# The decode rows' projection on four column strips in fp32, head norms in pairs, and attention's transfers later

## The reference

```
kv = einsum('btd,de->bte', rms_norm(x, g_kv), w_kv)      # 1024 x 3072: k and v of 3 groups, 8 heads of 64
k, v = rotary(rms_norm(kv[:, :, 0], k_gain), pos), kv[:, :, 1]
q = einsum('btd,de->bte', rms_norm(x, g), w_q)           # 1024 x 1536
q = rotary(rms_norm(q, q_gain), pos) * 64 ** -0.5        # rms_norm here is over each head of 64
o_g, lse_g = softmax attention of group g: windows 128, 512, 2048, dilations 1, 4, 16
o = sum_g softmax_g(lse_g) * o_g;  x = x + o @ w_o
```

## Time and profile before

| | |
|---|---|
| median of three runs | 2099.83 us |
| the profiled execution | 2097.21 us, span 2095.4 us |
| its mean granted TensorE clock | 0.993 of full speed |
| TensorE's busy share of the span | 99% |
| chain that ended last, share on TensorE | 92% (VectorE 4%, DMA 1%, ScalarE 1%) |
| HBM traffic | 303.02 MB read, 172.30 MB written |

### The profile page before, as it was taken

The page is one execution under the profiler, slowest core; times in us unless marked ns, Lnnn a source line. Parts: engine busy times, 40 slices in busy tenths (PEclk is TensorE's granted clock), DMA queues, the critical chain, the costliest instruction groups (busy, mean ns, idle before and its releaser), DMA issues.

```text
span 2095.4 us, 44747 instructions
## 1 busy us (share of the span) xinstructions
PE 2065.7 (99%) x17325; PEld 2011.4 (96%) x17325; DVE 1596.1 (76%) x2141; ACT 1083.3 (52%) x1963; POOL 562.9 (27%) x630
## 2 busy tenths in 40 slices
PE   8999999999999999999999899999999999999998
PEld 8999999999999999999999767899999999999998
DVE  5888888888755787867868697788888888875544
ACT  5655555455544665455554456555555555553332
POOL 1002232322210254635546203620132322321000
PEclk8999999999999999999999999999999999999999
DMA  6235777788998632453534785122676878899664
GB/s 209 82 102 160 201 188 208 192 198 213 302 291 261 204 121 91 129 158 108 188 127 143 238 242 200 35 92 86 166 194 193 211 187 213 191 300 295 195 207 141
DMA packets 264468, 380.67 MB, mean 182 GB/s; under 512 B 23511, under 2 KB 161399, under 8 KB 262438
## 3 DMA queue, kind: packets, MB, share of 16 engines
q1 hardware_dynamic: 227670, 281.35, 41.5%
q0 software_dynamic: 31376, 92.79, 20.3%
q10 hardware_dynamic: 5288, 4.68, 0.7%
HBM read 303.02 MB, written 172.30 MB: 227 GB/s over the span
## 4 chain that ended last, share of the span: by engine, by line
PE 92%; DVE 4%; DMA 1%; ACT 1%; issue 1%; POOL 0%; SPq 0%; ACTq 0%; DVEq 0%; POOLq 0%
PE ps L1290 42%; PE ps L1393 21%; PE ps L2607 5%; PE ps L2609 5%; PE ps L2610 5%; PE ps L2861 2%; PE ps L2924 2%; PE ps L2626 2%; PE ps L2960 1%; PE ps L2939 1%; PE ps L446 1%; PE ps L889 1%; PE ps L2887 1%; PE ps L512 1%; PE ps L2916 1%; DMA chin<-in_state_conv 1%
## 5 line engine op out<-in xcount | busy, mean ns | idle before, releaser
L1290 PE MATMUL ps<-hT,w 128*128 128x258 f32 x2752 | 458.3, 283 | 0.5 <-DVE ua L1523 0.5
L1290 PEld LDWEIGHTS ps<-hT,w 128*128 128x128 f32 x2752 | 384.9, 189 | 1.2 <-issue 0.6
L1290 PE MATMUL ps<-lT,w 128*128 128x258 f32 x1376 | 276.2, 282 | 0.0
L1290 PE MATMUL ps<-hB,w 128*128 128x258 f32 x1344 | 229.4, 282 | 0.0
L1290 PEld LDWEIGHTS ps<-lT,w 128*128 128x128 f32 x1376 | 213.3, 189 | 0.0
L1393 PE MATMUL ps<-gdh,wda 128*128 128x258 f32 x1184 | 198.8, 283 | 0.0
L1393 PE MATMUL ps<-gdh,wdb 128*128 128x258 f32 x1152 | 193.4, 284 | 0.0
L1290 PEld LDWEIGHTS ps<-hB,w 128*128 128x128 f32 x1344 | 191.0, 189 | 0.0
L1393 PEld LDWEIGHTS ps<-gdh,wda 128*128 128x128 f32 x1184 | 166.8, 190 | 0.3
L1393 PEld LDWEIGHTS ps<-gdh,wdb 128*128 128x128 f32 x1152 | 161.7, 189 | 0.8 <-issue 0.2
L2607 PE MATMUL ps<-ring,xhS 128*128 128x256 f32 x560 | 157.8, 282 | 0.0
(11 more groups left out here) (414 smaller groups left out, 5579.5 us busy)
## 6 DMA issues: line engine op xcount, KB each, us to landing
stage<-in_w_up SPq DMA_DIRECT2D x176, 256.0 KB, 3.6
wsum<-in_w_down POOLq DMA_DIRECT2D x132, 256.0 KB, 5.3
gs<-cb SPq DMA_DIRECT2D x44, 516.0 KB, 6.9
stage<-wsum SPq DMA_DIRECT2D x88, 256.0 KB, 3.3
tsum<-gs POOLq DMA_DIRECT2D x66, 258.0 KB, 7.5
tsum<-gneg POOLq DMA_DIRECT2D x66, 258.0 KB, 8.5
stage<-in_w_down SPq DMA_DIRECT2D x58, 256.0 KB, 3.4
kvs<-stage SPq DMA_DIRECT2D x24, 512.0 KB, 4.4
```

Source lines behind the costliest of these rows:

```text
L1290: mm = pe.matmul(ps[:, bank + c, 0:HB], w, m[:, c * HB:(c + 1) * HB], start=(first and i == 0), stop=(i == len(parts) - 1), skip_group_che ...
```

## The change

Four parts.

1. The samples' rows are multiplied in plain fp32: xs and xs12 hold the 8 rows once, and the moving operand is the scaled but unsplit weights in their own buffers (`raw`). The four 128-row parts of a block go to four column strips (`strip_products`), so one block is 4 matmuls of 32x256, and each strip keeps its own partial sum. `samples_first` does B11 ahead of that product, `samples` does B21, T3 and B22 together behind T1 (in step 0 behind B21). ScalarE copies the strips out (`act_strips`), `fold_samples` adds them on TensorE by four matmuls with a summing matrix inside product T3, and VectorE copies 4 pieces (`dve_sample_rows`). Since `raw` is read by the matmuls, the sum T1 of step n now waits for the B11 strips (`samples_begun`), and the load of the next B12 for all strips.
2. Norms are done in pairs: c11 and c22 share floor, root and the four small operations, so do c12 and c21. The scaling of the first of a pair moves behind the second's sum.
3. In the last step the first q tile is copied earlier and the masks are built later.
4. In attention, loads of cache rows (`V_AT`) are spread over s = 3 to 13 in place of 2 to 9 and 13; copies of k/v rows to outputs move from s = 4 on to s = 16 on, the loads of x from s = 10 on to s = 14 on; `sp_new_rows` is cut in two, and its loads for the samples move from s = 3 to s = 4.

```diff
@@ -2270,11 +2293,23 @@
             wait(act, pj_cs, 2 * n - 1)
             act_wide(act, two(rb[:, 0:T]), ps[:, 2:4, :], (pj_pe, nth(n, "T3")))
 
-        def act_sample_low(act, n):
-            act.wait_ge(pj_ss, n + 3)
-            row_free(act, n, "S")
-            wait(act, pj_k, 2 * n)
-            nc.scalar.activation(knS[:, :], ps[32:XS, 6 + n % 2, :], ACT.Copy).then_inc(pj_k, 1)
+        def samples_done(n):
+            return (pj_ss, 3 * n + 3)
+
+        def samples_folded(n):
+            return (pj_ss, 3 * n + 4)
+
+        def samples_begun(n):
+            return (pj_ss, 3 * n + 2)
+
+        def kept_strips(n):
+            return xb12[:, 0:QW] if n == LASTP else strips[:, :]
+
+        def act_strips(act, n):
+            act.wait_ge(*samples_done(n))
+            if n == LASTP:
+                act.wait_ge(pj_l, nth(n, "T3"))
+            nc.scalar.activation(kept_strips(n), ps[:, 6 + n % 2, :], ACT.Copy).then_inc(pj_xh, 1)
 
         def act_project(act):
             def act_x_his(name):
...
@@ -2363,32 +2396,39 @@
             row_free(v, n, "c12")
             nc.vector.tensor_tensor(two(row(n, "c12")), ps[:, 4:6, :], two(acc[:, 0:T]), ALU.add).then_inc(pj_cs, 1)
 
-        def dve_sample_add(v, n):
-            v.wait_ge(pj_k, 2 * n + 1)
-            nc.vector.tensor_tensor(knS[:, :], knS[:, :], ps[0:NS, 6 + n % 2, :], ALU.add).then_inc(pj_k, 1)
+        def dve_sample_rows(v, n):
+            v.wait_ge(*samples_folded(n))
+            row_free(v, n, "S")
+            for q in range(4):
+                ins = nc.vector.tensor_copy(knS[:, q * P:(q + 1) * P], ps[32 * q:32 * q + NS, 6 + n % 2, q * P:(q + 1) * P])
+            ins.then_inc(pj_k, 1)
 
...
@@ -2440,29 +2479,33 @@
                     if before:
                         dve_mean(v, n - 1, "c12")
                         dve_lo(v, n, "B21")
-                        dve_normed(v, n - 1, "c12")
-                        dve_sample_add(v, n - 1)
+                        dve_sample_rows(v, n - 1)
                         dve_lo(v, n, "T3")
                         if last:
                             dve_weights_sum(v, n, "T4")
                         dve_mean(v, n - 1, "c21")
+                        dve_floor(v, n - 1, "near")
+                        if last:
+                            dve_lo(v, n, "T4")
+                        else:
+                            dve_lo(v, n + 1, "B11")
+                        dve_factor(v, n - 1, "near")
+                        dve_normed(v, n - 1, "c12")
+                        dve_mean(v, n - 1, "S")
+                        dve_floor(v, n - 1, "rows")
                         dve_normed(v, n - 1, "c21")
                         if last:
-                            dve_lo(v, n, "T4")
-                        dve_mean(v, n - 1, "S")
-                        if not last:
-                            dve_lo(v, n + 1, "B11")
+                            dve_first_queries(v)
+                        dve_factor(v, n - 1, "rows")
                         dve_normed(v, n - 1, "S")
                         if not normed:
                             sample_scores(v, gi, 0)
...
@@ -2473,31 +2516,31 @@
                     dve_weights_sum(v, n + 1, "T1")
                 if normed:
                     dve_mean(v, n, "c11")
-                    dve_normed(v, n, "c11")
                 dve_c22p(v, n)
                 if not last:
                     dve_weights_sum(v, n, "T4")
                     dve_lo(v, n, "T4")
                 if n == 0:
                     dve_x_los("A22")
-                if last:
-                    v.wait_ge(at_tp, 1)
-                    nc.vector.tensor_scalar(qT[:, 0, :], ps[:, 7, :], gq[:, 0:1], None, ALU.mult).then_inc(at_tc, 1)
                 if normed:
                     dve_mean(v, n, "c22")
+                    dve_floor(v, n, "far")
+                    dve_factor(v, n, "far")
+                    dve_normed(v, n, "c11")
                     dve_normed(v, n, "c22")
                 else:
                     dve_values(v, n, "c22")
                 if last:
                     v.wait_ge(at_tp, 2)
                     nc.vector.tensor_copy(kT[:, 0, :], ps[:, 7, :]).then_inc(at_tc, 1)
+                    dve_masks(v)
...
-            def samples(n, b):
-
-                rows = {"B11": xs[:, 0:KH, :], "B21": xs[:, KH:KC, :], "T3": xs[:, 0:KH, :], "B22": xs12[:, :, :]}[b]
-                h, first = (0 if b in ("B11", "B21") else 1), b in ("B11", "T3")
-                w = wslot(n, b)
-                pe.wait_ge(pj_l, nth(n, b))
-                if b == "B11" and n:
-                    pe.wait_ge(*((pj_k, 2 * n - 2) if n > 1 else (pj_s, 2)))
+            def strip_products(n, b, rows, h, moving):
+                for k in range(KH):
+                    mm = pe.matmul(ps[32 * k:32 * k + XS, 6 + n % 2, h * CW:(h + 1) * CW], rows[:, k, :],
+                                   moving[:, k * CW:(k + 1) * CW], start=(b == "B11"), stop=(b in ("B21", "B22")),
+                                   tile_position=(0, 32 * k), skip_group_check=True)
+                return mm
+
+            def samples_first(n):
+
                 if n == 0:
-                    pe.wait_ge(pj_xs, {"B11": 3, "B21": 5, "T3": 3, "B22": 6}[b])
-                for k in range(KH):
-                    for i in range(2):
-                        mm = pe.matmul(ps[0:XS, 6 + n % 2, h * CW:(h + 1) * CW], rows[:, k, :], w[:, i, k * CW:(k + 1) * CW],
-                                       start=(b == "B11" and k == 0 and i == 0), stop=(not first and k == KH - 1 and i == 1),
-                                       skip_group_check=True)
-                if b == "B22":
-                    mm.then_inc(pj_ss, 1)
-                return mm
+                    pe.wait_ge(pj_xh, 1)
+                    pe.wait_ge(pj_l, nth(0, "B11"))
+                    w = wslot(0, "B11")
+                    strip_products(0, "B11", xs[:, 0:KH, :], 0, w[:, 0, :].bitcast(F32))
+                    mm = strip_products(0, "low", xs[:, 0:KH, :], 0, w[:, 1, :].bitcast(F32))
+                else:
+                    pe.wait_ge(*scaled_by(n, "B11"))
+                    pe.wait_ge(*((pj_k, n - 1) if n > 1 else (pj_s, 2)))
+                    mm = strip_products(n, "B11", xs[:, 0:KH, :], 0, raw(n, "B11"))
+                mm.then_inc(pj_ss, 1)
+
+            def samples(n):
+                if n == 0:
+                    pe.wait_ge(pj_xh, 2)
+                    pe.wait_ge(pj_xs, 4)
+                pe.wait_ge(*scaled_by(n, "B21"))
+                pe.wait_ge(*weights_summed(n, "T3"))
+                strip_products(n, "B21", xs[:, KH:KC, :], 0, raw(n, "B21"))
+                strip_products(n, "T3", xs[:, 0:KH, :], 1, raw(n, "T3"))
+                strip_products(n, "B22", xs12, 1, raw(n, "B22")).then_inc(pj_ss, 1)
+
+            def fold_samples(n):
+                pe.wait_ge(pj_xh, 2 + n + 1)
+                for q in range(4):
+                    mm = pe.matmul(ps[32 * q:32 * q + NS, 6 + n % 2, q * P:(q + 1) * P], fold[:, :],
+                                   kept_strips(n)[:, q * P:(q + 1) * P], start=True, stop=True, tile_position=(0, 32 * q),
+                                   skip_group_check=True)
+                mm.then_inc(pj_ss, 1)
 
             pe.wait_ge(f_xa, 6 * KH + 1)
             product(0, "B11")
             pe.wait_ge(f_xa, 7 * KH)
             for c in range(2):
                 pe.matmul(ps[:, 2 + c, :], xq["A11"][0][:, 0, 0:P], pre0[:, 0, 0:QW], start=True, stop=True)
-            samples(0, "B11").then_inc(pj_ss, 1)
+            samples_first(0)
             for n in range(LASTP + 1):
                 wait(pe, pj_cs, 2 * n)
                 product(n, "T1")
@@ -2645,18 +2708,19 @@
                         nm = pe.matmul(ps[0:MT[i], 7, i:i + 1], acc[:, i * P:i * P + MT[i]], ones[:, 0:1],
                                        start=True, stop=True)
                     nm.then_inc(pj_ss, 1)
+                if n:
+                    samples(n)
                 pe.wait_ge(pj_cp, 5 * n + 1)
                 product(n, "T2")
-                samples(n, "B21")
                 product(n, "B21")
-                samples(n, "T3")
+                if n == 0:
+                    samples(n)
                 pe.wait_ge(pj_cp, 5 * n + 2)
-                product(n, "T3")
+                product(n, "T3", third=lambda: fold_samples(n))
                 if n < LASTP:
-                    samples(n + 1, "B11")
+                    samples_first(n + 1)
                     pe.wait_ge(pj_cp, 5 * n + 3)
                     product(n + 1, "B11")
-                    samples(n, "B22")
                     pe.wait_ge(pj_cs, 2 * n + 1)
                     product(n, "B22")
                     pe.wait_ge(pj_cp, 5 * n + 4)
@@ -2665,14 +2729,8 @@
...
@@ -2769,19 +2830,21 @@
                     load_sample(sp, GROUPS - 1, 6)
                     load_sample(sp, GROUPS - 1, 7)
                 if s == 3:
```

(17 more changed lines are left out.)

140 lines of the change are left out of this document (77 added, 63 removed).

## The result

| | median of 5 runs | range | profiled execution |
|---|---|---|---|
| before | 2099.83 us | 2099.12 to 2101.85 | 2097.2 us (span 2095.4) |
| changed | 2121.80 us | 2119.56 to 2124.69 | 2119.56 us (span 2117.8) |

The ratio is 1.0106, with an interval of 1.0092 to 1.0121. The forecast was 2092.1 us, 2083 to 2104: wrong in sign, and outside its range.

The account below looks back on a forecast made before the run. TensorE, busy in 99% of the span, was taken as the bound. The terms -8.2 + 6.5 - 1.0 - 5.0 = -7.7 us took the median from 2099.8 to 2092.1 us, with a range of 2083 to 2104.

Parts of the forecast that it names:

- Part 1, the strips: TensorE in the projections: strip blocks and folds cost 25.7 us against 33.8 for the old blocks, -8.2; bounds -15 to +8.
- 0.7, 1.6 and 0.5: TensorE's prices in us per projection step: `samples_first` 0.7, `samples` 1.6, the fold 0.5.
- R+42.2: In a k step, R being the start of T1, TensorE ends T4 42.2 us later.
- The rule weighed there: Column strips share a row group, so each round would wait for its weight loads; the forecast's trace left 0.10 us.
- Part 2, the later norms: Projections: blocks leave later, so reused slots and late weights delay TensorE, +6.5 us; bounds 0 to +22.
- VectorE waits for the B11 strips (25.3): In a k step VectorE waits until 25.3 us after T1's start, then does sums and norms; c11 scaled at 36.3 to 37.6.
- +0.7, +1.5, +0.7, +1.3 and +2.3: TensorE's waits in us: c21's slot in steps 1, 4 and 7, then late c12 and B22 weights in steps 2 and 5.
- Part 3, the turn: Turn to attention: wait for VectorE's first q copy goes, -1.5; four 8x128 copies, +0.5; sum -1.0 us, from -1.5 to +1.
- it lands just as B22 ends: 0: At the turn, c11 of step 8 is stored later but frees the slot c21 needs in time, costing 0.
- Part 4: Attention's transfers: the 3.6 us wait for a q tile goes, and 1.4 of slow matmuls behind it; -5.0 us, -6.5 to 0.
- it meets no wait at 14 to 22: Attention's moved copies fall into 1283 to 1340 us, where no DMA wait was seen; a wait there would make the term 0.
- Rival 3: c21's slot and late B22 weights hold TensorE over 3 us in five steps, the clock falls, +22: 2107.6 us; chance 0.13.

Follow-up runs that it names:

- run 11: Run 5 with run 9's order on SP and VectorE's sum for sample 4 moved into the next step: 2087.85 us, ratio 0.9942.
- run 4: The changed kernel with norms block by block again; strips, early first q copy, late masks and attention's transfers kept: 2103.32 us, ratio 1.0023.
- run 5: Run 4 with VectorE's sum T1 of the next step put behind its lo part of T4: 2090.14 us, ratio 0.9952.
- run 6: The changed kernel with VectorE's sum T1 put behind the lo part of T4: 2112.62 us, ratio 1.0059.
- run 8: The changed kernel with four stage slots in place of three, the fourth over the convolution's history: 2125.96 us, ratio 1.0128.
- run 10: The changed kernel with run 9's order on SyncE and run 8's four slots together: 2121.10 us, ratio 1.0102.
- run 14: The changed kernel with four slots, c21's store behind the weights, and VectorE's sums of the samples' products left out: 2099.97 us, ratio 1.0004.
- run 3: The kernel before with attention's transfers moved alone: 2092.96 us, ratio 0.9972.
- run 2: The kernel before with norms in pairs, early first q copy and late masks; old samples and attention's transfers kept: 2115.45 us, ratio 1.0083.
- run 9: The changed kernel with c21's store put behind the B22 and B21 weight loads on SyncE in v steps 2 and 5: 2119.78 us, ratio 1.0090.
- run 12: Run 6 with run 9's order on SyncE: 2109.93 us, ratio 1.0047.
- run 7: The changed kernel with c21's store behind the B22 and B21 weight loads in v steps 2 and 5, sample rows 2 and 3 behind it: 2115.46 us, ratio 1.0078.
- run 16: Run 11 with VectorE's sums for samples 2 and 3 moved later as well: 2093.88 us, ratio 0.9973.

## Why the prediction was wrong, step by step

**Part 1, the strips: -8.2 forecast.** The prices were right. A first block and what follows it, and a run of twelve calls with the last product matmul ahead, on TensorE's timeline of the changed kernel:

```profile
795.98 0.64 PE L2659 MATMUL ps<-xodd,xs 128*32 128x256 f32 x8
796.55 0.39 PE L2650 MATMUL ps<-ring,xhA 128*128 128x256 f32 x1
...
863.88 0.28 PE L2653 MATMUL ps<-ring,xlS 128*128 128x256 f32 x1
864.09 1.50 PE L2659 MATMUL ps<-xb,xs 128*32 128x256 f32 x24
```

From distances between neighbours: 0.66, 1.53, and 0.43 for the fold, against 0.7, 1.6 and 0.5. Four old blocks took 3.74 of a step, the new ones take 2.62. From T1 to T1 steps 1 to 7 still fell only from a mean of 43.62 to 42.98 in run 11, where the waits are gone, since the products took 0.48 more; 0.64 x 9 = -5.8, and run 11's stage is 6.7 shorter. So the term was mis-sized by some 2 us: the products beside the blocks were taken as before, and a step that the prediction ends at R+42.2 took 43.0 undisturbed.

The rule weighed there, that column strips cannot hide each other's weight loads (the Trainium skill, "TensorE: Matmul & The Clock Gate", The mechanism), is not borne out: the loads of a round of four start beside the running matmuls of the round before (from 864.33 us, beside matmuls that run from 864.33 to 864.71), and twelve calls end within 1.5 us. What a drain at a change of tiling (the Trainium skill, "TensorEngine Tiling (Array Packing)", Key Properties) can have cost is small: 0.21 us from the last product matmul's start to the strips in place of the usual 0.12.

**Part 2, the later norms: +6.5 forecast. This is where it failed**, in two steps.

The first is "VectorE waits for the B11 strips (25.3)". The prediction used that wait only for the time at which c11 is scaled. It did not follow what else is queued behind it on VectorE for TensorE's own use: c22's sum, sum T4 and the lo parts. It is worth 12.5 us (run 4 less run 5) to 13.2 (change less run 6), and belongs to the strips, not to the norms.

The second is the sum over +0.7, +1.5, +0.7, +1.3 and +2.3. It came to 16.8 us in five waits. The times up to VectorE were close: in step 1 (R = 814.6) c11's scaling was over at R+38.8 (forecast 36.3 to 37.6), in step 2 (R = 858.2) c12's began at R+21.2 (19). Each step after that was longer. GpSimd took 8.8 us for c11 in place of 6.8, and c21's copy came at R+50.9 in place of 47 to 48.5. c21's store ended at R+37 in place of 33, the B22 weights were issued at R+39.6 in place of 34.5 and landed after 7.0 in place of 6 (the DMA share was 1.03 from 897 to 905 us, where the mean of a step had been 0.40). So T2 waited 2.0, 3.8 and 2.1, and T1 4.0 and 5.0. Each extra microsecond passed to TensorE whole, as the forecast lay on the edge. And the third queue, VectorE in line for GpSimd's products of the samples, was not in the prediction at all; before, that wait was there (10.0 us in six places over the stage) and cost nothing.

**Part 3, the turn: -1.0 forecast, +8.7 measured.** The 1.5 us went, as said (that wait stood inside T4 of step 8, so it counts in the projections above). The step "it lands just as B22 ends: 0" failed: ScalarE waited 17.1 us for c11's slot of step 8, c21 of that step was copied at 1185.2, and the first scores waited 3.9 us. The lower clock did the rest, for 13.7 us. How much of the turn is the slot's and how much VectorE's queue stays open: with four slots (runs 8, 10 and 14) the first scores still wait 2.0, 2.0 and 1.6 us, the next copy of q 7.5, 7.1 and 3.9, and no run with the pairs has a turn under 14.0. ScalarE's row in the changed kernel:

```profile
1185.17 1.57 ACT L2271 ACTIVATE stage<-ps,rtok 128x256 f32<-128x256 f32 x4 [17.15 <-DMA kvs<-stage]
```

**Part 4: -5.0 forecast, -5.0 measured** in the change (29.6 to 24.6), -6.3 in the median of run 3. That it meets no wait at 14 to 22 held in the change itself (0.3 us for the statistics) and not in runs 3, 4, 5, 6 and 11 (3.1 us each, in part by GpSimd's multiply, as above).

**Rival 3** had the pairs' mechanism and 0.13. It priced the waits and the clock at 22; they cost 22.2 + 5.8 = 28.0 in the stage and 8.7 at the turn. The strips' wait on VectorE and the queue for the samples' products are not in it either, and its 2107.6 is 14 us short. Its condition, that five waits pass 14.2 us together, was met with 16.8, though the stores from 840 to 900 us landed after 2.9 to 3.5 us and not after the 5.9 that it asked for; GpSimd's time and the weights' landing were the long terms. It was held improbable for one median landing time and a mean DMA share. The chance should have followed from the count of queues: with several in-order queues each within 2 us of being late, the short end of each is needed, not the middle.

## What to carry to other kernels

A wait put at the head of an in-order queue is priced by everything behind it that the bounding engine needs, not only by the result that the wait guards; list that queue to its end. When removing one wait gains nothing, look for the next queue before discarding the theory: here three changes worth 0.6, 4.0 and 3.9 us of the stage alone were worth 24.8 together. Work on an engine that isn't the bound is free only while its slack lasts; here the saving of 60 small operations on VectorE (2141 to 2081 in run 2) cost 16 us, because it moved results later.

## What the runs showed of the hardware

The granted clock is not a function of the wait alone: TensorE's wait of 2.0 us ahead of T2 of step 2 was followed by no fall in the changed kernel and by one in run 9, at the same place, and waits of 3.5 and 3.6 us (runs 10 and 12) by none, where a wait of 3.6 in run 7 and each of those of 3.8 us and more in the projections was. The fall after T2 of step 5 made 120 product matmuls take 15.8 us in place of 14.3.

A 128x512 fp32 scalar copy for the strips took 0.59 us and four copies of 8x128 1.18 us on VectorE, as long as one 128x1024 sum. GpSimd's multiply by the gains of 128x1024 took 2.4 or 3.4 us in the same kernel; each time that VectorE scaled a block and summed c12 beside it, it took 3.4 (why is not shown). The other way round, VectorE's subtraction of 128x24 took 2.34 us in run 11, where a multiply of GpSimd's was running, and 0.18 in run 16, where it began ahead of that multiply.
